# Five small edits to a two-block kernel: the last norm's totals, the keys' head sums, the gated outputs' split, a layer norm's mean, and gathered rows in the last inner units

## The chip, the cores and the metric

The kernel runs on one core of one Trainium2 chip. The metric is the device time of one execution in microseconds (us); lower is better. A core has five engines: TensorE (PE in the profile, with its weight loads as PEld), VectorE (DVE), ScalarE (ACT), GpSimd (POOL) and SyncE (SP, which here only issues loads and stores). Every engine runs its own list of instructions in order, and the engines wait for one another at semaphores.

## The reference

Two transformer blocks are applied to 256 tokens of width 2048, in float32:

```python
def first_block(x, mem, ...):      # one layer
    # k, v of memory = mem_n @ w_kv; rms norm of each of the 4 heads of q and of k; attention over 256 memory rows
    # gated delta rule on the projections; gates by silu; (gated outputs) @ w_out; residual
    ...
def second_block(x, ...):
    mix = jnp.concatenate([out_pool, out_attn], axis=-1) @ w_out[l]
    h = layer_norm(ALPHA * h + mix, ln1_g[l], ln1_b[l])
    ffn = peer_ffn(h, peer_wq[l], peer_subkeys[l], peer_u[l], peer_v[l])
    h = layer_norm(ALPHA * h + ffn, ln2_g[l], ln2_b[l])
```

`peer_ffn` lets every token choose experts by the sums of two top-k scores; a chosen expert contributes gelu(x·u) times its gate times its row v. The changed places are the norm of the memory's keys (`xa_k_norm_g`), the gated outputs ahead of `w_out`, the norm ln1, the last units of the products with u, and the norm ln2 that ends the kernel.

## The kernel before, in words

All weights come as 466 **units** of 128 x 2048 float32 (1 MB each), which SyncE loads into rotating buffers (`raw`). Float32 accuracy is kept by splitting: for each half unit ACT rounds 128 x 1024 values to a high part (`WH`, `cast`, L2619) and DVE subtracts that from the original to get the low part (`WL`, L1838). The activations are split in the same way, and PE forms three products, WH·XH, WH·XL and WL·XH (all at L1178). `do("prep", q)` splits half unit q; inside `unit` the half that is split is three halves ahead of the one that PE multiplies.

The class `Plan` writes one order of steps, and each engine emits its own part of each step, so that the order in `Plan.run` is the order on every engine. Side work is a generator that is advanced between the parts of a unit; `together(side, units, n)` advances both in turn. What a step waits for is written as `wait_ge(*at(name, count))`.

The places that the change touches, in order of time:

- **Memory's keys and values.** Units KV to KV+7 give the 8 key tiles, KV+8 to KV+15 the 8 value tiles. `head_norm("k")` runs beside the value units: `hn_square` (GpSimd multiplies 128 x 2048 keys by themselves, L3013), `hn_sum` (32 PE products 128 x 64 with a constant add the squares up; DVE takes the reciprocal of the root that ACT forms), `hn_spread`, `hn_apply`. `mv_root` is another small PE step after the second value unit.
- **Gated outputs.** Nine steps `y_split(c)` split 32 tiles of 128 x 256 in chunks of 2 to 4 tiles (`CHUNKS`; ACT casts L2795, DVE subtracts L2157) ahead of the units WO. The first chunk holds tiles 0 to 3, in the order in which WO's first unit uses them. The splits of half units that were asked for earlier stand behind these steps on both engines.
- **ln1.** `ln1` forms the mean MU and the reciprocal deviation RS of 256 tokens, and the product MR of both. `h2(c)` (c = 0 to 8) normalizes two of 16 row blocks a step (128 x 512): DVE multiplies by RS (L2307) and subtracts MR (L2309), ACT applies gain and bias (L2600) and casts (L2869), and one step later DVE subtracts the low part (L2313). Ahead of the steps stands `prep(2*WQ)` with the split of a half of unit WQ+1. The first two units of WQ follow as a pair.
- **PEER.** 192 of the 256 tokens take part in dense products over all experts: two halves, each with 64 inner units (u) and 64 outer units (v, `vm`). The last 64 tokens are done by rows that are gathered: `sp_gather(k)` is an indirect DMA of 128 rows, 1 MB, issued by GpSimd (L3197) into one of two buffers, and `sp_use(k)` a DVE operation 128 x 2048 on it (L1829 for the rows of v). `sp_gather(k)` waits for `sp_use(k-2)`. `pace` advances this side work by 0.13 or 0.05 of a step per part of an inner unit, and 0.27 or 0.3 per half of an outer unit (first or second half of PEER). An inner unit has 8 such parts. `c_begin(1)`, after the last inner unit, lets GpSimd issue three loads, 2 MB of the stored h and 1 MB each of ln2's gain and bias; they share one queue with the gathers.
- **End.** The two groups of 128 tokens (t = 0, 1) lie in `OUT[0]`, `OUT[1]`. For t = 0, DVE adds the four PSUM banks, ACT sums each row by a pass over the four parts (L2601); for t = 1 the rows of the last 64 tokens are brought to their place by 8 PE products, DVE copies the 64 others, ACT sums again. The mean goes to DVE, a pass `Square` with its row sum follows on ACT for each t, then one root of both (with an ACT table load before it), one reciprocal, and on DVE eight passes 128 x 1024 that subtract the mean, scale, and apply gain LG and bias LB. ACT and SyncE each issue two of the four output DMAs.

Of the kernel before, what the change touches and what calls it, by code (L numbers as in the profile page):

```python
# [149 lines left out]
CHUNKS = [list(range(4)), list(range(4, 8)), [10, 12, 14, 16], [18, 20, 22, 24], [26, 28, 30], [11, 13, 15, 17],  # L150
# [48 lines left out]
class Plan:  # L199
# [364 lines left out]
    def peer(self, half, st):  # L564
# [3 lines left out]
        for j in range(64):  # L568
# [5 lines left out]
            for _ in self.unit(PEER + 128 * half + j, per=6, later=later if half == 0 and j >= 62 else None):  # L574
# [9 lines left out]
                if half or j < 61:  # L584
                    self.pace(st, 2 * half)
# [32 lines left out]
    def run(self):  # L618
# [8 lines left out]
        for c in range(9):  # L627
            do("y_split", c)
# [43 lines left out]
        do("prep", 2 * WQ)  # L672
        for c in range(9):
            do("h2", c)
        do("sub_load")
# [24 lines left out]
def gate_counts():  # L700
# [14 lines left out]
    "x_high": (("n_hi", 32), ("y_hi", 9), ("x1_hi", 8), ("att_hi", 8), ("pm_hi", 8), ("h2_hi", 8)),  # L715
    "x_low": (("n_lo", 32), ("y_lo", 9), ("x1_lo", 8), ("att_lo", 8), ("pm_lo", 8), ("h2_lo", 8)),
# [35 lines left out]
def build(nc, D, out, scratch):  # L752
    ctx = ExitStack()
    with ctx:
# [30 lines left out]
        def f(kb, n):  # L785
            return view(kb, n, F)
# [245 lines left out]
        CM, MU, RS, MR = f(80, 256), f(81, 256), f(82, 256), f(83, 256)  # L1032
# [75 lines left out]
        def sync_program(e):  # L1108
# [51 lines left out]
            def end():  # L1160
                for p in range(2):
                    s.wait_ge(*at("out_t", 2 * p + 2))
# [661 lines left out]
        def vector_program(e):  # L1824
# [467 lines left out]
            def ln1():  # L2292
# [8 lines left out]
                v.wait_ge(*at("ln1_rs", 1))  # L2301
                v.step(tt(MR, MU, RS, ALU.mult))
# [153 lines left out]
            def sp_sum():  # L2456
# [6 lines left out]
                v.step(stt(x, HN[LAST, 2048:4096], ALPHA, x, ALU.mult, ALU.add))  # L2463
# [84 lines left out]
            def end():  # L2548
# [19 lines left out]
                v.wait_ge(*at("y2_sd", 1))  # L2568
                v.step(recip(stat(16, 2), stat(14, 2)))
                v.wait_ge(*at("ld_ln2", 32))  # L2570
                v.wait_ge(*at("y2_mean", 2))
                for t in range(2):
                    for c in range(2):
                        o = slice(1024 * c, 1024 * c + 1024)
                        x = OUT[t][:, o]
                        v.own()
                        v.step(stt(x, x, stat(10 + t), LG[:, o], ALU.add, ALU.mult))
                        v.own()
                        stt(x, x, stat(16 + t), LB[:, o], ALU.mult, ALU.add).then_inc(S["out_t"], 1)
# [15 lines left out]
        def scalar_program(e):  # L2595
# [378 lines left out]
            def end():  # L2974
                for t in range(2):
                    for d in range(4):
                        o = slice(d * 512, d * 512 + 512)
                        a.wait_ge(*at("y2", 4 * t + d + 1))
                        act(HN[:, t * 2048 + d * 512:t * 2048 + d * 512 + 512], OUT[t][:, o], ACT.Identity,
                            acc=stat(4 * t + d)).then_inc(S["y2_sum"], 1)  # L2980
                    a.wait_ge(*at("y2_mean", t + 1))
                    a.step(act(HN[:, t * 2048:t * 2048 + 2048], OUT[t], ACT.Square, bias=stat(10 + t), acc=stat(12 + t)))
                a.own()
# [332 lines left out]
```

## Time and profile before

| | |
|---|---|
| time, median of 3 runs | 2832.28 us (2826.26 to 2835.13) |
| profiled execution | 2836.36 us, of which the span from the first to the last instruction is 2834.5 us |
| PE busy | 2733.1 us, 96% of the span |
| DVE / ACT / POOL busy | 1929.7 us (68%) / 1384.3 us (49%) / 389.4 us (14%) |
| mean granted TensorE clock | 0.987 |
| PE's share of the chain that ended last | 73% (DVE 13%, DMA 7%, ACT 5%) |

PE's busy time is the sum of its matmul instructions; the rest of the span is idle time of PE, and the tail in which no product is left. The granted clock is the mean over the stretch of the clock that the chip gave TensorE, as a share of 2.4 GHz. A matmul in a stretch at 0.5 takes about twice as long. In timelines the time in brackets is the idle time of that engine just before the row, and behind the arrow stands what the profile infers to have ended it.

### The profile page before, as it was taken

How to read it: one execution, taken by the hardware profiler on the slowest of the kernel's cores; microseconds unless marked ns; L12 is line 12 of the kernel's file. 1: busy time of each engine (PE TensorE's matmuls, PEld its weight loads, DVE VectorE, ACT ScalarE, POOL GpSimd, SP SyncE). 2: the span in 40 equal slices, each digit the busy share in tenths (PEclk: the TensorE clock that was granted, in tenths of full speed). 3: DMA queues.
4: the chain of work that ended last, by engine and by line, in shares of the span. 5: the costliest groups of instructions: out<-in, count | busy, mean ns of one | idle time of the engine just before them, and what ended most of it. 6: DMA issues, size and time to landing. Idle time of an engine off the chain costs nothing.

```text
span 2834.5 us, 43483 instructions
## 1 busy us (share of the span) xinstructions
PE 2733.1 (96%) x17934; PEld 2557.6 (90%) x17934; DVE 1929.7 (68%) x2867; ACT 1384.3 (49%) x2255; POOL 389.4 (14%) x366
## 2 busy tenths in 40 slices
PE   8999989889999999999999999999999999999996
PEld 8899989889998889979989999998888999988885
DVE  7456578544445455564669657767888888878986
ACT  6356454556555444444453133435555555555554
POOL 0100020211110000005000012221222111113210
PEclk9999999999999999999999999999999999999998
DMA  6444455433335554544544579999999988899993
GB/s 256 163 150 163 149 164 185 140 104 117 102 114 193 193 181 166 189 157 151 179 149 149 202 268 346 359 346 366 377 378 380 345 319 322 324 353 367 371 365 123
DMA packets 109669, 668.28 MB, mean 236 GB/s; under 512 B 25777, under 2 KB 26313, under 8 KB 31553
## 3 DMA queue, kind: packets, MB, share of 16 engines
q1 hardware_dynamic: 83808, 496.08, 48.4%
q0 software_dynamic: 24512, 164.97, 16.0%
q10 hardware_dynamic: 1152, 4.47, 0.4%
q8 instruction: 142, 2.33, 0.3%
q14 instruction: 55, 0.44, 0.0%
HBM read 651.54 MB, written 13.30 MB: 235 GB/s over the span
## 4 chain that ended last, share of the span: by engine, by line
PE 73%; DVE 13%; DMA 7%; ACT 5%; issue 2%; POOL 0%; DVEq 0%; ACTq 0%
PE PS L1178 72%; DMA m<-in_pun,keep 4%; DVE WL L1838 4%; DVE m L1829 3%; ACT WH L2619 2%; DMA m<-in_pv,keep 1%; ACT m L2600 1%; PE PS L1181 1%; DVE m L2084 1%; ACT m L2601 1%; DMA m<-s_kk 1%; DVE m L2081 1%; PE PS L1556 0%; ACT L2600 0%; DVE m L2440 0%
## 5 line engine op out<-in xcount | busy, mean ns | idle before, releaser
L1838 DVE TENSOR_TENSOR WL<-raw,WH 128x1024 fp32r<-128x1024 f32 x708 | 869.0, 1233 | 544.8 <-ACT WH L2619 543.5
L2619 ACT CAST WH<-raw 128x1024 fp32r<-128x1024 f32 x708 | 736.8, 1046 | 393.5 <-PE PS L1178 381.0
L1178 PE MATMUL PS<-m_4096r,WH 128*128 128x256 f32 x4672 | 881.4, 289 | 12.1 <-DVE m L1829 5.2
L1178 PEld LDWEIGHTS PS<-m_4096r,WH 128*128 128x128 f32 x4672 | 734.3, 193 | 17.8 <-DVE m L1829 6.0
L1178 PE MATMUL PS<-m_4096r,WL 128*128 128x256 f32 x2336 | 663.6, 284 | 0.0
L1178 PE MATMUL PS<-WH,m_896r 128*128 128x512 f32 x1536 | 516.6, 390 | 6.5 <-DVE m_896r L2533 3.1
L1178 PEld LDWEIGHTS PS<-m_4096r,WL 128*128 128x128 f32 x2336 | 450.0, 193 | 0.0
L1178 PE MATMUL PS<-WL,m_896r 128*128 128x512 f32 x1024 | 399.1, 390 | 0.0
L1178 PE MATMUL PS<-m_8192r,WH 128*128 128x384 f32 (+1 forms) x1536 | 373.1, 331 | 8.2 <-issue 2.7
L1178 PEld LDWEIGHTS PS<-WH,m_896r 128*128 128x128 f32 x1536 | 289.0, 188 | 68.2 <-DVE m_896r L2533 4.2
L1178 PE MATMUL PS<-m,raw 128*128 128x192 f32 x2048 | 342.0, 326 | 0.0
L1178 PEld LDWEIGHTS PS<-m,raw 128*128 128x128 f32 x2048 | 331.6, 190 | 0.3 <-issue 0.2
L1178 PE MATMUL PS<-m_8192r,WL 128*128 128x192 f32 (+1 forms) x1280 | 258.8, 267 | 0.0
L1178 PEld LDWEIGHTS PS<-m_8192r,WH 128*128 128x128 f32 x1536 | 236.5, 193 | 10.4 <-issue 3.1
L1178 PEld LDWEIGHTS PS<-m_8192r,WL 128*128 128x128 f32 x1280 | 235.8, 190 | 0.0
L1178 PEld LDWEIGHTS PS<-WL,m_896r 128*128 128x128 f32 x1024 | 192.6, 188 | 39.9
L1178 PE MATMUL PS<-m 128*128 128x128 f32 (+2 forms) x1360 | 199.7, 285 | 27.8 <-ACT m L2600 18.1
L1178 PEld LDWEIGHTS PS<-m 128*128 128x128 f32 x1360 | 178.8, 194 | 34.0 <-ACT m L2600 19.5
L2440 DVE SCALAR_TENSOR_TENSOR m<-m 128x2048 f32<-128x2048 f32 x64 | 146.4, 2288 | 50.9 <-DMA m<-in_pun,keep 50.9
L3197 POOL DMA_INDIRECT m<-in_pv,keep x64 | 111.1, 1736 | 488.4 <-DVE m L1829 470.4
L1178 PE MATMUL PS<-WH,m_8192r 128*128 128x512 f32 x512 | 159.3, 392 | 2.7 <-issue 2.7
L1829 DVE SCALAR_TENSOR_TENSOR m<-m,keep 128x2048 f32<-128x2048 f32 (+1 forms) x67 | 152.9, 2283 | 7.5 <-DMA m<-in_pv,keep 7.2
(266 smaller groups left out, 2627.8 us busy)
## 6 DMA issues: line engine op xcount, KB each, us to landing
raw<-in_pu SPq DMA_DIRECT2D x112, 1024.0 KB, 7.1
raw<-in_pv SPq DMA_DIRECT2D x96, 1024.0 KB, 8.9
raw<-in_w_qkv SPq DMA_DIRECT2D x48, 1024.0 KB, 4.8
raw<-in_w_o SPq DMA_DIRECT2D x48, 1024.0 KB, 4.8
raw<-in_w SPq DMA_DIRECT2D x40, 1024.0 KB, 4.8
raw<-in_w_z SPq DMA_DIRECT2D x32, 1024.0 KB, 4.8
m<-in_pv SPq DMA_DIRECT2D x32, 1024.0 KB, 8.9
raw<-in_w_kv SPq DMA_DIRECT2D x16, 1024.0 KB, 5.2
```

The lines of the kernel that those rows point to most:

```text
L1178: return e.matmul(o, l, x, start=start, stop=stop)
L1181: return e.transpose(o, i, C("ident"))
L1829: return e.scalar_tensor_tensor(out=o, in0=a, scalar=s, in1=b, op0=op0, op1=op1)
L1838: tt(WL[:, k, :], raw_of(n)[:, h * 1024:h * 1024 + 1024], WH[:, k, :].bitcast(F), ALU.subtract).then_inc(S["lo"], 1)
L2081: v.step(tt(tmp, iv_u[:, :, c, j:j + 1].broadcast_to(shape), iv_e[:, 0:2, j:j + 1, r].broadcast_to(shape), ALU.mult))
L2084: t = tt(iv_u[:, :, c, r], iv_u[:, :, c, r], tmp, ALU.subtract)
L2440: x = e.scalar_tensor_tensor(out=g, in0=g, scalar=1.0, in1=XS, op0=ALU.mult, op1=ALU.mult, accum_out=DOT[:, r:r + 1])
L2600: return e.activation(o, i, fn, scale=scale, bias=bias)
L2601: return e.activation(o, i, fn, scale=scale, bias=bias, accum_out=acc)
L2619: e.copy(WH[:, k, :], raw_of(n)[:, h * 1024:h * 1024 + 1024]).then_inc(S["hi"], 1)
L3197: e.indirect_dma_start(out=GB[b], out_offset=None, in_=D["pun" if k < 64 else "pv"], in_offset=bass.IndirectOffsetOnAxis(ap=EI[:, r:r + 1] ...
```

## The change

The five edits:

- **Sums at the end (`end`).** For t = 0 the DVE additions also give the row sums; for t = 1 ACT copies the 64 rows out of PSUM and sums them, and the last 64 rows' sums come from the step that forms them (`sp_sum`). The root's table is loaded ahead by an operation on a constant, each t has its own root and reciprocal, and the second half of t = 1 is scaled by ACT and finished by GpSimd (times LG, plus LB), which SyncE's last store waits for.
- **Keys' head sums (`head_norm`).** For the keys two more `yield`s stand ahead of `hn_sum`, so that it and the steps after it come 8 parts, two units, later.
- **Gated outputs (`CHUNKS`).** Tiles 0 to 3 are split in three chunks of 1, 1 and 2 tiles rather than in one.
- **ln1's mean (`ln1`, `h2`).** GpSimd subtracts MU (a step per 128 x 512), DVE then multiplies by RS; MR is no longer formed. `prep(2*WQ)` stands behind `h2(3)` rather than ahead of `h2(0)`.
- **Gathered rows (`peer`).** In the inner units 61 to 63 of the second half `pace` is no longer called, as was already so in the first half.

```diff
-CHUNKS = [list(range(4)), list(range(4, 8)), [10, 12, 14, 16], [18, 20, 22, 24], [26, 28, 30], [11, 13, 15, 17],
+CHUNKS = [[0], [1], [2, 3], list(range(4, 8)), [10, 12, 14, 16], [18, 20, 22, 24], [26, 28, 30], [11, 13, 15, 17],
           [19, 21, 23, 25], [27, 29, 31], [8, 9]]
...
         self.do("hn_square", which)
         yield
         yield
+        if which == "k":
+            yield
+            yield
         self.do("hn_sum", which)
...
-                if half or j < 61:
+                if j < 61:
                     self.pace(st, 2 * half)
...
         do("ln1")
-        do("prep", 2 * WQ)
         for c in range(9):
             do("h2", c)
+            if c == 3:
+                do("prep", 2 * WQ)
...
             def h2(c):
                 if c < 8:
                     x = k3(X1)[:, 2 * c:2 * c + 2, :]
-                    a = v.step(tt(x, x, bc(RS, 2), ALU.mult))
-                    v.own(a)
-                    tt(x, x, bc(MR, 2), ALU.subtract).then_inc(S["h2_norm"], 1)
+                    v.wait_ge(*at("ln1_rs", 1))
+                    v.wait_ge(*at("h2_mean", c + 1))
+                    tt(x, x, bc(RS, 2), ALU.mult).then_inc(S["h2_norm"], 1)
...
+            def h2(c):
+                if c == 8:
+                    return
+                g_.wait_ge(*at("ln1_mu", 1))
+                x = k3(X1)[:, 2 * c:2 * c + 2, :]
+                tt(x, x, bc(MU, 2), ALU.subtract).then_inc(S["h2_mean"], 1)
...
                 v.wait_ge(*at("used", done(NUNIT - 1)))
+                for d in range(4):
+                    x = OUT[0][:, d * 512:d * 512 + 512]
+                    v.step(e.scalar_tensor_tensor(out=x, in0=x, scalar=1.0, in1=PS[:, d, :], op0=ALU.mult, op1=ALU.add,
+                                                  accum_out=stat(d)))
                 for t in range(2):
-                    for d in range(4):
-                        x = OUT[t][:, d * 512:d * 512 + 512]
-                        if t == 0:
-                            tt(x, x, PS[:, d, :], ALU.add).then_inc(S["y2"], 1)
-                        else:
-                            v.wait_ge(*at("folded", d + 1))
-                            copy(x[0:64, :], PS[0:64, 4 + d, :]).then_inc(S["y2"], 1)
-                    v.wait_ge(*at("y2_sum", 4 * t + 4))
+                    if t:
+                        v.wait_ge(*at("y2_copy", 4))
+                    v.own()
...
+                v.wait_ge(*at("y2_sd", 1))
+                v.step(recip(stat(16), stat(14)))
+                scaled(0, 0)
+                v.wait_ge(*at("y2_sd", 2))
+                v.step(recip(stat(17), stat(15)))
+                v.own()
+                tt(stat(18), stat(11), stat(17), ALU.mult).then_inc(S["y2_shift"], 1)
+                scaled(0, 1)
+                scaled(1, 0)
...
             def end():
+                act(stat(20), C("eps5"), ACT.Sqrt).then_inc(S["y2_table"], 1)
+                for d in range(4):
+                    a.wait_ge(*at("folded", d + 1))
+                    act(OUT[1][0:64, d * 512:d * 512 + 512], PS[0:64, 4 + d, :], ACT.Identity,
+                        acc=STAT[0:64, 4 + d:5 + d]).then_inc(S["y2_copy"], 1)
                 for t in range(2):
...
                     a.wait_ge(*at("y2_mean", t + 1))
                     a.step(act(HN[:, t * 2048:t * 2048 + 2048], OUT[t], ACT.Square, bias=stat(10 + t), acc=stat(12 + t)))
...
+                a.wait_ge(*at("y2_shift", 1))
+                act(OUT[1][:, 1024:2048], OUT[1][:, 1024:2048], ACT.Identity, scale=stat(17),
+                    bias=stat(18)).then_inc(S["y2_scaled"], 1)
...
+            def end():
+                x = OUT[1][:, 1024:2048]
+                g_.wait_ge(*at("y2_scaled", 1))
+                g_.wait_ge(*at("ld_ln2", 32))
+                g_.step(tt(x, x, LG[:, 1024:2048], ALU.mult))
+                g_.own()
+                tt(x, x, LB[:, 1024:2048], ALU.add).then_inc(S["out_pool"], 1)
```

How this moves instructions. On PE, after the products of the second value unit (`WH`, `WL` with the keys' and values' inputs in `m_4096r`), the head sums of the keys are the row with a constant and 128 x 64; before:

```order
L1178 MATMUL PS<-WH,m_4096r 128x512 x2
L1178 MATMUL PS<-WL,m_4096r 128x512
L1178 MATMUL PS<-cons,m_2048 128x64 x16
L1181 MATMUL PS<-cons,m_256 128x128 x2
L1178 MATMUL PS<-WH,m_4096r 128x512 x2
L1178 MATMUL PS<-WL,m_4096r 128x512
```

and of the change, at the same place:

```order
L1182 MATMUL PS<-WL,m_4096r 128x512
L1182 MATMUL PS<-WH,m_4096r 128x512 x2
L1182 MATMUL PS<-WL,m_4096r 128x512
L1185 MATMUL PS<-cons,m_256 128x128 x2
L1182 MATMUL PS<-WH,m_4096r 128x512 x2
L1182 MATMUL PS<-WL,m_4096r 128x512
```

The row with 128 x 64 is gone from here and stands two units of products further on, while the step `mv_root` (128 x 128) stays. On DVE, in ln1 and h2 (x is `m_4096`, MU, RS and MR are `m_256`), before:

```order
L2300 RECIPROCAL m_256<-m_256 128x256
L2302 TENSOR_TENSOR m_256<-m_256 128x256
L1838 TENSOR_TENSOR WL<-raw,WH 128x1024
L2307 TENSOR_TENSOR m_4096<-m_4096,m_256 128x512
L2309 TENSOR_TENSOR m_4096<-m_4096,m_256 128x512
L2307 TENSOR_TENSOR m_4096<-m_4096,m_256 128x512
L2309 TENSOR_TENSOR m_4096<-m_4096,m_256 128x512
L2313 TENSOR_TENSOR m_8192r<-m_4096,m_8192r 128x512
```

and of the change:

```order
L2304 RECIPROCAL m_256<-m_256 128x256
L2311 TENSOR_TENSOR m_4096<-m_4096,m_256 128x512 x2
L2315 TENSOR_TENSOR m_8192r<-m_4096,m_8192r 128x512
L2311 TENSOR_TENSOR m_4096<-m_4096,m_256 128x512
L2315 TENSOR_TENSOR m_8192r<-m_4096,m_8192r 128x512
L2311 TENSOR_TENSOR m_4096<-m_4096,m_256 128x512
L2315 TENSOR_TENSOR m_8192r<-m_4096,m_8192r 128x512
L1842 TENSOR_TENSOR WL<-raw,WH 128x1024
L2311 TENSOR_TENSOR m_4096<-m_4096,m_256 128x512
```

One DVE operation of two per piece is gone, and the weight split stands behind the fourth multiplication, ahead of the fourth low part. On GpSimd, around the three loads of `c_begin(1)` (`in_pv` rows are the gathers), before and of the change:

```order
L3197 DMA m_2048<-in_pv,keep 128x2048 x26
L3227 DMA m_4096<-s_h 128x4096
L3228 DMA m_2048<-in_ln2g 128x2048
L3229 DMA m_2048<-in_ln2b 128x2048
L3197 DMA m_2048<-in_pv,keep 128x2048 x30
```

```order
L3218 DMA m_2048<-in_pv,keep 128x2048 x24
L3248 DMA m_4096<-s_h 128x4096
L3249 DMA m_2048<-in_ln2g 128x2048
L3250 DMA m_2048<-in_ln2b 128x2048
L3218 DMA m_2048<-in_pv,keep 128x2048 x32
```

Two gathers that stood ahead of the three loads now stand behind them in the queue.

## Rows read from the trace of the kernel before

**Rows 1.** Part 1 of the page: busy time, share of the span, instructions.

```profile
PE 2733.1 (96%) x17934; PEld 2557.6 (90%) x17934; DVE 1929.7 (68%) x2867; ACT 1384.3 (49%) x2255; POOL 389.4 (14%) x366
```

**Rows 2.** Timeline of PE, rows with idle time: start, us, instruction, [idle before].

```profile
78.53 6.84 PE L1178 MATMUL PS<-cons,m 128*128 128x64 f32 x32 [3.38 <-POOL m L3013]
...
867.41 1.19 PE L1178 MATMUL PS<-WH,m_8192r 128*128 128x512 f32 x2 [2.71 <-issue]
...
1433.48 0.48 PE L1178 MATMUL PS<-m_8192r,WH 128*128 128x256 f32 x2 [2.71 <-issue]
...
2512.90 0.80 PE L1178 MATMUL PS<-WH,m_896r 128*128 128x512 f32 x1 [2.75 <-DVE cons L2525]
...
2543.94 0.50 PE L1178 MATMUL PS<-WH,m_896r 128*128 128x512 f32 x1 [2.11 <-DVE m_896r L2533]
```

**Rows 3.** Stretches: us; busy PE, PEld, DVE, ACT, POOL (count); PEclk; DMA share; GB/s.

```profile
78.91:89.15 10.24, 10.24 (x42) 9.47 (x42) 1.51 (x3) 1.20 (x2) 0.00 (x0) 0.50 0.08 10
...
1434.00:1437.40 3.40, 3.40 (x18) 3.40 (x18) 3.35 (x6) 2.74 (x6) 0.00 (x0) 0.51 0.00 0
```

**Rows 4.** Timeline of PE: the same 32 products for the queries.

```profile
184.65 3.68 PE L1178 MATMUL PS<-cons,m 128*128 128x64 f32 x32
```

**Rows 5.** Timelines of POOL and DVE around GpSimd's two multiplications 128 x 2048.

```profile
70.57 7.91 POOL L3013 TENSOR_TENSOR m<-m 128x2048 f32<-128x2048 f32 x1 [70.12 <-DVE m L1901]
...
70.39 4.62 DVE L1838 TENSOR_TENSOR WL<-raw,WH 128x1024 fp32r<-128x1024 f32 x4
...
175.94 3.60 POOL L3013 TENSOR_TENSOR m<-m 128x2048 f32<-128x2048 f32 x1 [97.46 <-ACT m L2680]
...
176.84 3.78 DVE L1838 TENSOR_TENSOR WL<-raw,WH 128x1024 fp32r<-128x1024 f32 x1 [1.87 <-ACT WH L2619]
```

**Rows 6.** Timelines of ACT and DVE ahead of unit WO.

```profile
865.01 7.76 ACT L2795 CAST m_8192r<-m 128x1024 fp32r<-128x1024 f32 x9
...
866.08 9.24 DVE L2157 TENSOR_TENSOR m_8192r<-m,m_8192r 128x1024 fp32r<-128x1024 f32 x9 [1.87 <-ACT m_8192r L2795]
875.24 4.63 DVE L1838 TENSOR_TENSOR WL<-raw,WH 128x1024 fp32r<-128x1024 f32 x4
```

**Rows 7.** Timeline of DVE in h2: the early split, the first and the last low part.

```profile
1428.34 1.22 DVE L1838 TENSOR_TENSOR WL<-raw,WH 128x1024 fp32r<-128x1024 f32 x1
...
1432.69 0.69 DVE L2313 TENSOR_TENSOR m_8192r<-m,m_8192r 128x512 fp32r<-128x512 f32 x1 [0.48 <-ACT m_8192r L2869]
...
1446.18 0.69 DVE L2313 TENSOR_TENSOR m_8192r<-m,m_8192r 128x512 fp32r<-128x512 f32 x1 [1.21 <-ACT m_8192r L2869]
```

**Rows 8.** GpSimd's groups: count, busy us, mean ns, idle before and its releaser.

```profile
L3040 POOL TENSOR_TENSOR m<-m,m 128x512 f32<-128x512 f32 x12 | 15.3, 1278 | 49.5 <-ACT m L2600 49.5
```

**Rows 9.** Timelines of DVE and POOL, then DMA issues 2480 to 2580 us (count, size, us to landing).

```profile
2541.27 2.35 DVE L1829 SCALAR_TENSOR_TENSOR m<-m,keep 128x2048 f32<-128x2048 f32 x1 [3.83 <-DMA m<-in_pv,keep]
...
2524.45 1.73 POOL L3197 DMA_INDIRECT m<-in_pv,keep  x1 [8.85 <-DVE m L1829]
...
m<-s_h POOLq DMA_DIRECT2D x1, 2048.0 KB, 11.1
...
m<-in_ln2b POOLq DMA_DIRECT2D x1, 1024.0 KB, 21.2
```

**Rows 10.** Timelines of PE, ACT and DVE at the end.

```profile
2808.57 3.65 PE L1178 MATMUL PS<-m,cons 128*64 128x512 f32 x8
...
2817.33 2.00 ACT L2601 ACTIVATE m<-m,keep 128x2048 f32<-128x2048 f32 x1 [0.41 <-DVE keep L1832]
...
2819.44 1.28 ACT L2600 ACT_TABLE_LOAD   x1
2820.73 0.29 ACT L2600 ACTIVATE keep<-keep,cons 128x2 f32<-128x2 f32 x1
...
2821.36 5.12 DVE L1829 SCALAR_TENSOR_TENSOR m<-m,keep,m 128x1024 f32<-128x1024 f32 x4
2826.40 5.12 DVE L1829 SCALAR_TENSOR_TENSOR m<-m,keep 128x1024 f32<-128x1024 f32 x4
```

More of the change, by code:

```diff
@@ L626, in run @@
         self.mix()
-        for c in range(9):
+        for c in range(len(CHUNKS)):
             do("y_split", c)
@@ L1161, in end @@
                 for p in range(2):
-                    s.wait_ge(*at("out_t", 2 * p + 2))
+                    s.wait_ge(*at("out_pool", 1) if p else at("out_t", 2))
                     e.dma_start(out[0, tok(p), 1024:2048], OUT[p][:, 1024:2048]).then_inc(S["st_sync"], 16)
@@ L2462, in sp_sum @@
                 v.wait_ge(*at("ld_hn", 16))
-                v.step(stt(x, HN[LAST, 2048:4096], ALPHA, x, ALU.mult, ALU.add))
+                v.step(e.scalar_tensor_tensor(out=x, in0=HN[LAST, 2048:4096], scalar=ALPHA, in1=x, op0=ALU.mult, op1=ALU.add,
+                                              accum_out=STAT[LAST, 4:5]))
+                v.step(copy(STAT[LAST, 5:8], C("zero")[LAST, 0:3]))
             count = {"gelu": 0, "gated": 0, "apply": 0}
@@ L2567, in end, with scaled @@
                     one(stat(10 + t), stat(8 + t), -1.0 / 2048, ALU.mult).then_inc(S["y2_mean"], 1)
-                v.wait_ge(*at("y2_sd", 1))
-                v.step(recip(stat(16, 2), stat(14, 2)))
                 v.wait_ge(*at("ld_ln2", 32))
                 v.wait_ge(*at("y2_mean", 2))
[L2572 to L2579, printed above, removed]
+                def scaled(t, c):
+                    o = slice(1024 * c, 1024 * c + 1024)
+                    x = OUT[t][:, o]
+                    v.own()
+                    v.step(stt(x, x, stat(10 + t), LG[:, o], ALU.add, ALU.mult))
+                    v.own()
+                    stt(x, x, stat(16 + t), LB[:, o], ALU.mult, ALU.add).then_inc(S["out_t"], 1)
+                v.wait_ge(*at("y2_sd", 1))
[3 more added lines that the diff above has]
+                v.step(recip(stat(17), stat(15)))
+                v.own()
+                tt(stat(18), stat(11), stat(17), ALU.mult).then_inc(S["y2_shift"], 1)
+                scaled(0, 1)
+                scaled(1, 0)
             Plan({"prep": prep, "begin": begin, "m_split": m_split, "n_add": n_add, "n_root": n_root, "n_scale": n_scale,
@@ L2974, in end @@
             def end():
-                for t in range(2):
[L2976 to L2980, printed above, removed]
+                act(stat(20), C("eps5"), ACT.Sqrt).then_inc(S["y2_table"], 1)
[3 more added lines that the diff above has]
+                        acc=STAT[0:64, 4 + d:5 + d]).then_inc(S["y2_copy"], 1)
+                for t in range(2):
                     a.wait_ge(*at("y2_mean", t + 1))
                     a.step(act(HN[:, t * 2048:t * 2048 + 2048], OUT[t], ACT.Square, bias=stat(10 + t), acc=stat(12 + t)))
-                a.own()
-                act(stat(14, 2), stat(12, 2), ACT.Sqrt, scale=1.0 / 2048, bias=C("eps5")).then_inc(S["y2_sd"], 1)
+                    a.own()
+                    act(stat(14 + t), stat(12 + t), ACT.Sqrt, scale=1.0 / 2048, bias=C("eps5")).then_inc(S["y2_sd"], 1)
+                a.wait_ge(*at("y2_shift", 1))
+                act(OUT[1][:, 1024:2048], OUT[1][:, 1024:2048], ACT.Identity, scale=stat(17),
+                    bias=stat(18)).then_inc(S["y2_scaled"], 1)
                 for t in range(2):
@@ L3114, in x_load @@
             def x_load():
-                g_.wait_ge(*at("y_lo", 9))
+                g_.wait_ge(*at("y_lo", len(CHUNKS)))
                 e.dma_start(f(120, 4096), D["x"]).then_inc(S["ld_res"], 16)
             def bias_load():
-                g_.wait_ge(*at("y_lo", 9))
+                g_.wait_ge(*at("y_lo", len(CHUNKS)))
                 g_.wait_ge(*at("used", done(KIWI - 1)))
@@ L3229, in c_begin @@
                 e.dma_start(LB, D["ln2b"]).then_inc(S["ld_ln2"], 16)
-            Plan({"hn_square": hn_square, "qk_out": qk_out, "iv_turn": iv_turn, "iv_store": iv_store,
+            def end():
[5 more added lines that the diff above has]
+                tt(x, x, LB[:, 1024:2048], ALU.add).then_inc(S["out_pool"], 1)
+            Plan({"end": end, "hn_square": hn_square, "qk_out": qk_out, "iv_turn": iv_turn, "iv_store": iv_store,
                   "iv_scale": iv_scale, "iv_out": iv_out, "dn_low": dn_low, "dn_y": dn_y, "gate": gate, "x_load": x_load, "bias_load": bias_load, "bias": bias, "ki_out": ki_out,
-                  "pool_loads": pool_loads, "pu_out": pu_out, "sub_load": sub_load, "h_store": h_store,
+                  "pool_loads": pool_loads, "pu_out": pu_out, "h2": h2, "sub_load": sub_load, "h_store": h_store,
                   "c_begin": c_begin, "s_add": s_add, "g_apply": g_apply, "gate_load": gate_load,
```

8 lines of the change are left out of this document (3 added, 5 removed).

## The prediction, made before the changed kernel had run

> **What bounds the kernel now.** I read the page's busy times first. PE is busy for 2733.1 us [rows 1], 96% of the span of 2834.5 us, and no edit takes a product away. So an edit can only pay where PE idles, where it runs at a low clock, or behind the last product. I then read PE's timeline at the changed places for idle time [rows 2]. PE waits 3.38 us ahead of the keys' head sums, 2.71 us ahead of the first product with the gated outputs, 2.71 us ahead of the first product of WQ, and 2.75 us after the last inner unit. A further gap of 2.11 us at 2543.94 is in the outer units, at a gathered row. Together that is 13.7 us.
>
> The clock adds to some of these. A table by stretches shows PE granted 0.50 from 78.91 to 89.15 and 0.51 from 1434.00 to 1437.40 [rows 3], which is the level of 1.2 GHz. At 2512.90 one product 128x512 takes 0.80 us, at 2543.94 the same product takes 0.50 [rows 2]: after the 2.75 us gap the clock was low, after the 2.11 us gap it was not. So a gap of nearly three microseconds costs its length and, when the clock falls with it, some 1.7 us more (half of the 3.40 us in rows 3).
>
> **Keys' head sums.** PE waits for GpSimd's multiplication, which takes 7.91 us because it runs beside four DVE subtractions [rows 5]. It ends at 78.48, and 78.53 is when the 32 products start [rows 2]. Moved two units, the sums are asked for about 11 us later (two units of products, an estimate of 5 to 6 us each from the timeline ahead), at some 86 us, so 3.38 us of wait go. The cover is the weights split already: DVE finishes four half units by 75.01 (70.39 + 4.62, rows 5), and these are what PE multiplies in place of the sums. The 32 products take 6.84 us at half clock [rows 2]; the queries' same 32 take 3.68 us at full clock [rows 4]. That is 3.16 us. The stretch at half clock runs on to 89.15 [rows 3]: from 85.4 on, 3.7 us of ordinary products that would take half, some 1.7 us less. Sum +8.2 us. The low bound is 3.4 us, if the 32 short products bring the clock down wherever they stand; rows 4 speak against that. High bound 8.5. What is late next: the reciprocal, the spread and the scaled keys, two units later; nothing reads them before the attention over memory, behind all value units. On DVE the reciprocal waits with the next weight split behind it, for the 4 us that the sums and the root take; the split is three halves ahead, so this is hidden.
>
> **Gated outputs.** Nine casts take 7.76 us and nine subtractions 9.24 us [rows 6], or 0.86 and 1.03 each, so the first chunk of four tiles costs 1.9 us before PE can start at 867.41. A quarter of it would take about 0.6 us, so PE starts some 1.3 us earlier. But the low part that the second half of WO's second unit needs is among the four subtractions that start at 875.24 [rows 6], behind all chunks on DVE. The tiles are the same 32, so DVE comes there at the same time, or 0.1 us later for two more instructions. PE gets there 1.3 us sooner and waits longer. I take 0. If the clock falls in that new wait, −1.7; if PE never catches up with DVE there, +1.3.
>
> **ln1's mean.** Before, DVE does three operations 128x512 per piece, and low parts come every 1.93 us (1432.69 to 1446.18, seven steps, rows 7). Of the change DVE does two, 2 x 0.69 = 1.38, and GpSimd one. GpSimd's nearest row is 128x512 in 1.28 us [rows 8]. Can the two overlap? Rows 5 say no. The multiplication that ran beside four subtractions took 7.91 us, the one that ran with one waiting took 3.60 us; the difference of 4.3 is about the time of the subtractions, and the one that waited took 3.78 us where such a one takes 1.22 [rows 7]. Then a piece costs 1.28 + 1.38 = 2.66 us, 0.73 more than before. GpSimd starts when the mean is there, ahead of DVE's reciprocal, so I count three of the eight pieces as done ahead: 5 x 0.73 = 3.7 us later. Against it, 1.22 us of the split and one 0.69 us operation no longer stand ahead of the first low part: 1.9 us sooner. The split is now behind the fourth piece, where the low part of that piece queues behind it on DVE while it waits for ACT's cast; PE will show a gap there, but the pieces behind come from GpSimd's head start. I take −1.8 us. Bounds: all eight pieces later and the split in full, 5.8 + 1.2 − 1.9 = −5.1; with no exclusion, +1.9 less what the split gives back, so +1.5.
>
> **Gathered rows.** Without the row ahead of the last inner unit's sum (a DVE operation of 2.35 us, as in rows 9), the gap of 2.75 us shrinks to about 0.8 and the clock should hold: 1.9 + 1.6 = +3.5 us. But the 24 parts are 1.2 steps of the side work, and two gathers now stand behind 4 MB of loads in GpSimd's queue. The last of these loads lands 21.2 us after its issue, and the gather issued at 2524.45 behind them landed only at 2541.27, 16.8 us later where the median is 10.1 [rows 9]. That cost DVE 3.83 us and PE 2.11 us. In the change a gather issued at about 2518 stands in that place, needed by about 2527 (the order puts this DVE operation in the fourth outer unit). It lands at 2533 to 2535, so DVE stalls for 6 to 7.5 us. Weight splits wait behind it, 1.5 units ahead; PE's gap, 2.11 before, would be 3.2 to 4.7, perhaps with the clock. That takes back 1 to 4.3 us. I take +0.5; bounds −2.5 and +3.5.
>
> **The end.** The last of eight DVE passes ends at 2831.52 (2826.40 + 5.12, rows 10), and 3.0 us more go to the last store. PE's last product ends at 2812.22. Of the change, ACT's last copy of 64x512 ends about 0.7 us behind that (a quarter of a 2.00 us pass and its readout). Then Square 2.1, root 0.3, reciprocal 0.2: 2815.6, where before the reciprocal came after both squares, the table load and the root, at 2821.06. Two passes at 1.27 (10.16 us for eight, rows 10) end at 2818.2. The second reciprocal and shift end at 2818.6, and ACT's scaling of 128x1024, half of 2.00, at 2819.8. What is left is four DVE passes, 5.1 us, and two GpSimd operations 128x1024. The latter are not in the trace: from 128x512 they are 2.56 us each [rows 8], from 128x2048 1.80 [rows 5]; I take 2.3, so 4.6. Each has two inputs from memory, as rows 5 have, so by those rows they exclude DVE's: 2818.6 + 5.1 + 4.6 = 2828.3. Gain +3.2 us. If they overlap, 2819.8 + 4.6 = 2824.4, gain 7.1; if GpSimd stretches 2.2 times, as 7.91 to 3.60, 2829.9, gain 1.6.
>
> The table load off the path is 1.28 us of this: the root starts at 2820.73, with nothing between it and the load [rows 10]. The Trainium skill (ScalarE: Activation LUTs, "What ACT_TABLE_LOAD costs") gives 1283 ns for the load, which this trace agrees with, and another 1380 ns for a drain, which it does not show. By the page the gain at the end would be an estimated 1.4 us larger.
>
> **Sum.** 8.2 + 0 − 1.8 + 0.5 + 3.2 = +10.1 us. The profiled execution took 2836.36 us, so it would take 2826.3. It lies 4.1 us above the median of 2832.28, inside the runs' 2826.26 to 2835.13; against the median the forecast is 2832.28 − 10.1 = 2822.2 us. Some 0.3%, 8.5 us, is what a measurement of this kernel can tell from no change.
>
> **Rivals.**
> - *Nothing excludes, and no new gap.* GpSimd's subtraction is hidden (+1.5), the end gains 7.1, the gathered rows 3.5, the gated outputs 1.3, the head sums 8.2: 21.6 at the most; with one of these missing, about 17, so 2815 us. For it: GpSimd is busy for 14% only. Against it: rows 5, twice.
> - *The late gather and the short products.* The 32 products bring their own low clock (gain 3.4 rather than 8.2), or the stall in the outer units takes all that the inner unit gave and 2.5 more. Either leaves 5 to 7 us, 2825 to 2827 us: no change that can be told. For it: a queue that answers in 16.8 us [rows 9]. Against it: rows 4.
> - *GpSimd stretched in ln1: slower than before.* If GpSimd's 1.28 us per piece stretches as in rows 5, to 2.8, and DVE's 1.38 comes on top, a piece takes 4.2 us: 8 x (4.2 − 1.93) − 1.9 = 16.3 us lost rather than 1.8, so the sum is −4.4, 2836.7 us. It decides from (10.1 + 1.8 + 1.9)/8 above 1.93, some 3.65 us per piece. For it: the 7.91 us. Against it: there DVE had four operations ready, in h2 it waits for GpSimd at each piece, so GpSimd finds the way free. The Trainium skill (GPSIMD Engine Reference, "Specifications") says that GpSimd's interfaces to the memory are shared with VectorE, and contended by instructions with two such inputs; the trace agrees by the 7.91 us, and that section puts no figure on it.
> - *The gated outputs' new wait* is in the terms already, by at most 1.7.
>
> **Chances and range.** My forecast, gains of 6 to 14 us, has 0.60; the large gain 0.13; the small gain 0.20; slower 0.07. Of the forecast's case some seven tenths lie above 8.5 us, so faster is 0.60 x 0.7 + 0.13 = 0.55; slower by over 0.3% needs the third rival with low clock in its gaps, 0.03; the rest is 0.42. The range runs from the large gain to the small one, 2814 to 2831 us.
>
> **What the trace will show.** Right: no gap at 74.9 us and granted clock 1.0 to 89 us, with 32 products in about 3.7 us near 86; PE starting on WO near 866 and waiting around 875; POOL rows of 1.3 us or more in h2 and low parts about 2.7 us apart, with one PE gap after the fourth piece; a gap under 1 us at the last inner unit and a longer one about four outer units later; a last DVE or POOL operation near 2828. Wrong: a low clock at the head sums in their new place; low parts under 2 us or over 3.6 us apart; DVE and POOL passes overlapping at the end; a gathered row that DVE does not wait for.

## The result, and the profile after

The changed kernel takes 2836.84 us in the median of 18 runs (2828.59 to 2846.58), the one before 2827.45 us over the 18 runs taken with and before it (2818.73 to 2835.13). The ratio is 1.0033, 95% interval 1.0024 to 1.0042: slower by 9.4 us, where 10 us faster was forecast. The three runs of before that the forecast had show a median of 2832.28 us, and its profiled execution, 2836.36 us, lies above all of these 18, and above the three runs' highest of 2835.13, where the prediction has it inside them. So the forecast counted from a time that was some 5 us too long: 10.1 us off the 2827.45 would have been 2817.4.

The profiled execution of the changed kernel has a span of 2836.8 us and took 2838.57 us. Its part 1 answers to [rows 1]:

```profile
PE 2733.8 (96%) x17934; PEld 2558.6 (90%) x17934; DVE 1932.6 (68%) x2862; ACT 1382.9 (49%) x2252; POOL 404.7 (14%) x376
```

Products and their time are the same, so all is in idle time, clock and tail. PE's timeline at the places of [rows 2], with idle time in brackets:

```profile
864.21 0.70 PE L1182 MATMUL PS<-WH,m_8192r 128*128 128x512 f32 x2 [1.61 <-issue]
...
874.41 0.73 PE L1182 MATMUL PS<-WH,m_8192r 128*128 128x512 f32 x2 [1.78 <-DVE WL L1842]
...
1432.72 0.76 PE L1182 MATMUL PS<-m_8192r,WH 128*128 128x256 f32 x2 [2.99 <-issue]
...
1441.84 0.50 PE L1182 MATMUL PS<-m_8192r,WH 128*128 128x256 f32 x2 [1.53 <-DVE m_8192r L2315]
...
2509.37 0.50 PE L1182 MATMUL PS<-WH,m_896r 128*128 128x512 f32 x1 [0.80 <-DVE cons L2529]
...
2540.22 0.79 PE L1182 MATMUL PS<-WH,m_896r 128*128 128x512 f32 x1 [7.88 <-DVE m_896r L2537]
```

The wait of 3.38 us at the keys' sums is gone, the gap after the last inner unit fell from 2.75 to 0.80 us, and the first product of WO starts after 1.61 us rather than 2.71. Against that stand new or longer gaps: 1.78 at 874.41, 1.53 at 1441.84, and 7.88 at 2540.22 where it was 2.11. The end is in DVE's and GpSimd's timelines and in the instructions of the program's last line (engine queue, operation: duration in ns, start in us):

```profile
2822.53 6.64 DVE L1833 SCALAR_TENSOR_TENSOR m<-m,keep 128x1024 f32<-128x1024 f32 x2
...
2821.46 3.35 POOL L3256 TENSOR_TENSOR m<-m 128x1024 f32<-128x1024 f32 x1 [46.41 <-ACT m L2611]
2824.90 3.19 POOL L3258 TENSOR_TENSOR m<-m 128x1024 f32<-128x1024 f32 x1
...
L758 POOLq DRAIN  x1: 11658/11658/11658, 2824.9 to 2824.9; - x1
L758 SPq DRAIN  x1: 7/7/7, 2832.3 to 2832.3; - x1
```

DVE's last pass ends at 2829.17, GpSimd's last operation at 2828.09, the last products' start being 1.65 us later than before. Counted from the last products' start, the passes are through 4 us sooner than in [rows 10]. But GpSimd's drain, the instruction behind its last operation, begins with that operation and ends at 2836.6, 8.5 us behind it. SyncE, the last of the others, was through at 2832.3; the span ends at 2836.8, with the drain. Before, its drain began at 2763.9 and was over long ahead of the end.

### The profile page after: what moved, and what is told of

It reads as the page before. It is cut to its first block, busy times and chain, and to the rows that moved or that the text cites. A ratio compares the mean times of both kernels' runs of the same rounds, so it can differ in the third digit from the quotient of the medians.

```text
span 2836.8 us, 43488 instructions
## 1 busy us (share of the span) xinstructions
PE 2733.8 (96%) x17934; PEld 2558.6 (90%) x17934; DVE 1932.6 (68%) x2862; ACT 1382.9 (49%) x2252; POOL 404.7 (14%) x376
## 4 chain that ended last, share of the span: by engine, by line
PE 80%; DVE 12%; ACT 5%; DMA 2%; issue 1%; POOL 0%; ACTq 0%; DVEq 0%
PE PS L1182 79%; DVE WL L1842 4%; DVE m L1833 2%; ACT WH L2630 2%; ACT m L2611 1%; PE PS L1185 1%; DMA m<-in_pv,keep 1%; DVE m L2088 1%; DMA m<-s_kk 1%; PE PS L1560 1%; DVE m L2085 1%; ACT L2611 0%; ACT m_4096r L2611 0%; ACT m L2612 0%; DVE m L2325 0%
## 5 line engine op out<-in xcount | busy, mean ns | idle before, releaser
L1833 DVE SCALAR_TENSOR_TENSOR m<-m,keep 128x2048 f32<-128x2048 f32 (+1 forms) x65 | 154.4, 2375 | 12.6 <-DMA m<-in_pv,keep 12.6
```

What stands on the lines that cost most here:

```text
L1833: return e.scalar_tensor_tensor(out=o, in0=a, scalar=s, in1=b, op0=op0, op1=op1)
```

## The experiments

Ratios are to runs of the kernel before beside them, with 95% intervals; 1.001 is 2.8 us. Stretches are taken from PE's timeline between the same products in each trace: they tell what one edit does to its own place more sharply than the whole time, which scatters by some 4 us between executions.

**The gathered rows alone, twice.**

```diff
-                if half or j < 61:
+                if j < 61:
                     self.pace(st, 2 * half)
```

> The kernel before with the edit on the gathered rows alone (no pacing in the inner units 61 to 63 of the second half). Theory 1 (the late gather is the loss): the gap of 2.75 us after the last inner unit shrinks to about 0.8 us, and a DVE operation on a gathered row waits about 10 us in the outer units, PE with it for 7 to 8 us where it was 2.11; 3 to 6 us slower than before, ratio 1.001 to 1.002. Rival (the late gather was one execution's accident): the stall is 4 us or less and the edit is 2 to 3.5 us faster.

> The edit on the gathered rows alone, again. Theory 1: a PE gap of 6 to 8 us some 30 us after the first outer product, in place of about 2 us, less the 1.95 us gained ahead of it: 1 to 4 us slower than before. Rival (the gained gap and clock pay for the late gather): 1 us slower to 2 us faster.

Ratios 1.0008 (0.9993 to 1.0024) and 0.9990 (0.9974 to 1.0006). Both profiles show the gap of 0.80 us ahead of the outer units and PE gaps of 6.39 and 6.62 us in them; from the first outer product to the last rows' products it takes 298.9 and 300.4 us, against a mean of 296.2 over twelve profiles of kernels without this edit (293.5 to 302.5). The mechanism of theory 1 is there both times. Its net cost, 1 to 2 us by the stretches (300.4 − 296.2, less the 1.95 us gained ahead, is the larger), is within the scatter of the whole times, so that 0 cannot be excluded.

**The gathered rows, with two of the loads later.**

```diff
+            if half and j in (12, 20):
+                self.do("ln2_load", j)
...
-                e.dma_start(LG, D["ln2g"]).then_inc(S["ld_ln2"], 16)
-                e.dma_start(LB, D["ln2b"]).then_inc(S["ld_ln2"], 16)
+            def ln2_load(j):
+                e.dma_start(*((LG, D["ln2g"]) if j == 12 else (LB, D["ln2b"]))).then_inc(S["ld_ln2"], 16)
```

> The kernel before with the edit on the gathered rows, and with the loads of the last norm's gain and bias (1 MB each) moved from the start of the outer units to the outer units 12 and 20; the 2 MB of h stay. Theory 1 (the gathers are late because 4 MB stand ahead of them in GpSimd's queue): PE's gap in the outer units, 6 to 8 us with the edit alone, falls to 2.5 us or less, and the kernel is 1 to 3 us faster than before. Rival (the two gathers themselves are late, whatever stands ahead): a gap of 5 us or more stays.

Ratio 0.9978 (0.9963 to 0.9993), some 6 us faster where 1 to 3 were expected. The gap at the late row is gone altogether, and the stretch is the shortest of all, 291.4 us. So the loads ahead in GpSimd's queue made the gathers late. How late, the changed kernel's GpSimd, DVE and DMA issues (2500 to 2560 us; size, us to landing) show: the gather issued at 2514.77, behind the three loads of 2508.87 to 2510.53, is used at 2536.41.

```profile
2509.97 0.56 POOL L3250 DMA_DIRECT2D m<-in_ln2b  x1
2514.77 1.73 POOL L3218 DMA_INDIRECT m<-in_pv,keep  x1 [4.25 <-DVE m L1833]
...
2536.41 2.35 DVE L1833 SCALAR_TENSOR_TENSOR m<-m,keep 128x2048 f32<-128x2048 f32 x1 [10.40 <-DMA m<-in_pv,keep]
...
m<-in_ln2b POOLq DMA_DIRECT2D x1, 1024.0 KB, 21.5
```

The three loads land 12.6, 17.0 and 21.5 us after their issues, at about 2521.5, 2526.4 and 2531.5, and the gather 4.9 us behind the last of them: one after the other in the order of issue, each of the last three MB some 5 us behind the one before. Before, too, the gather landed 5.1 us behind the third load (issued at 2515.02, landed 21.2 us later [rows 9]).

**The end alone, twice.** (The hunks of `end` and `sp_sum`.)

```diff
+                scaled(0, 1)
+                scaled(1, 0)
...
+                g_.step(tt(x, x, LG[:, 1024:2048], ALU.mult))
+                g_.own()
+                tt(x, x, LB[:, 1024:2048], ALU.add).then_inc(S["out_pool"], 1)
```

> The kernel before with the edits at the end alone (sums by additions, roots apart, GpSimd finishes the last quarter). Theory 1 (GpSimd's drain at the end eats the gain): DVE and GpSimd are done 23 us or less after the start of the eight products 128x512 that bring the last rows to their place, but the span ends only some 8 us after GpSimd's last operation, about 26.5 us after these products' start where it was 25.9; no change to 1 us slower. Rival: the drain is as short as it was in the kernel before, and the edit gains 2 to 3 us.

> The edits at the end alone, again. Theory 1 (nothing outside the tail): 0 to 3 us slower than before, and the time from the first outer unit's first product to the last products is that of the kernels without this edit, 294 to 299 us. Rival (the edit also slows the outer units): 5 us or more slower, and that time is 301 us or more, as in the first profile (302.5).

Ratios 1.0022 (1.0004 to 1.0039) and 1.0000 (0.9986 to 1.0014). The tail, from the start of the last rows' products to the end of the span, is 26.55 and 26.50 us, against 25.93 in the profiled kernel before. Theory 1 holds for the tail. The rival that the edit also slows the outer units fell: their stretch was 302.5 us in the first profile and 295.5 in the second.

**The end without GpSimd, twice.** DVE does the last quarter as a fourth `scaled` (the main lines against the kernel of the end alone; ACT's and GpSimd's parts of the last quarter go too).

```diff
-                tt(stat(18), stat(11), stat(17), ALU.mult).then_inc(S["y2_shift"], 1)
                 scaled(0, 1)
                 scaled(1, 0)
+                scaled(1, 1)
```

> The kernel before with the edits at the end, but without GpSimd: DVE does the last quarter too, ACT's scaling and GpSimd's step are left out. Theory 1 (GpSimd's drain costs about 8 us behind its last operation): the span ends some 20.5 us after the start of the eight products for the last rows, where it was 25.9 before and 26.6 with GpSimd. Rival (the passes themselves set the end, GpSimd's drain only fills a wait): DVE's two further passes bring the end to 26 us or more.

> The edits at the end without GpSimd, again. Theory 1 (nothing outside the tail): 4 to 7 us faster than before, 5 to 7 us faster than with GpSimd in this same call. Rival (the outer units are slowed too): 0 to 3 us faster.

Ratios 0.9968 (0.9954 to 0.9983) and 0.9976 (0.9965 to 0.9986); the tail is 20.44 us in both, 6.1 less than with GpSimd. Of these, some 4.3 us are the drain (from SyncE's 2832.3 to GpSimd's 2836.6 in the changed kernel) and the rest the slower passes. The wish to spare DVE two passes cost the whole gain of this edit.

**One short GpSimd addition behind the last pass.**

```diff
+            def end():
+                g_.wait_ge(*at("out_t", 4))
+                tt(stat(20), stat(0), stat(1), ALU.add).then_inc(S["tiny"], 1)
```

> The kernel before with one GpSimd addition of 128x1 behind the last DVE pass; its result is not used. Theory 1 (the drain is a fixed time of GpSimd after whatever it did last): the span ends about 8.5 us after this addition, 31 to 32 us after the start of the products for the last rows, where it was 25.9. Rival (the drain belonged to the long 128x1024 operations): the span ends at 26 to 27 us, with the last store.

The tail is 31.91 us, 6 more than before, for an addition of 0.20 us. GpSimd's timeline, and its drain in the last line's instructions:

```profile
2818.41 0.20 POOL L3233 TENSOR_TENSOR keep<-keep 128x1 f32<-128x1 f32 x1 [67.16 <-DVE m L1829]
...
L754 POOLq DRAIN  x1: 8662/8662/8662, 2818.4 to 2818.4; - x1
```

The drain ends 8.46 us behind the addition, as it ended 8.47 us (11.658 − 3.19) behind the long operation in the changed kernel: the length of the operation does not matter. It is not the same behind everything. Where GpSimd's last act is to issue a DMA, as in the kernel before, the drain ended 10.4 to 14.9 us behind that issue in 15 profiles, at 2783.9 at the latest, where it delays nothing.

**The keys' head sums alone.**

```diff
+        if which == "k":
+            yield
+            yield
         self.do("hn_sum", which)
```

> The kernel before with the keys' head sums two units later and nothing else. Theory 1: no wait at the sums and no low clock there, PE is 6 to 7 us further at 200 us, and stays so: 5 to 7 us faster, ratio about 0.998. Rival (the clock takes it back): PE's gaps after 390 us are the same, but the clock falls in more of them, and by 560 us the lead is 2 us or less; no change.

Ratio 1.0001 (0.9985 to 1.0018), neither as theory 1 nor by the rival's mechanism. The other profiles tell why. In e_end, whose code up to there is that of before, the same place reads (PE, then GpSimd and DVE):

```profile
75.05 3.79 PE L1178 MATMUL PS<-cons,m 128*128 128x64 f32 x32
...
70.48 4.51 POOL L3025 TENSOR_TENSOR m<-m 128x2048 f32<-128x2048 f32 x1 [70.03 <-DVE m L1901]
...
70.32 8.02 DVE L1838 TENSOR_TENSOR WL<-raw,WH 128x1024 fp32r<-128x1024 f32 x4
```

No wait, and no low clock: here DVE was held up (8.02 us for four subtractions, where [rows 5] have 4.62) and GpSimd came through in 4.51 us. In e_mean, again the old code at this place, GpSimd was held up as in the profile of before:

```profile
78.35 7.09 PE L1179 MATMUL PS<-cons,m 128*128 128x64 f32 x32 [3.39 <-POOL m L3012]
...
70.39 7.91 POOL L3012 TENSOR_TENSOR m<-m 128x2048 f32<-128x2048 f32 x1 [69.94 <-DVE m L1902]
```

Which of the two engines wins is settled anew in each execution: one and the same kernel gave 6.77 us for GpSimd in e_rows and 4.51 in e_rows_2, and 7.91 in e_mean and 4.51 in e_mean_2. Of 14 profiles with the old place of the sums, three have the wait of 3.4 us, one of 0.63 and ten none. The queries' sums behind it start at 184.1 to 184.7 us in the three, at 176.3 to 178.8 in the others, 178.9 in the mean; in six profiles with the new place at 177.2 to 177.8, 177.5 in the mean. By these means the edit is worth 1.4 us, not 8.2; the scatter of the 14 leaves it uncertain by some 2 us.

**The layer norm's mean alone, twice, and with the split left ahead.**

```diff
-        do("prep", 2 * WQ)
         for c in range(9):
             do("h2", c)
+            if c == 3:
+                do("prep", 2 * WQ)
```

> The kernel before with the layer norm's mean by GpSimd and the split moved, nothing else. Theory 1 (GpSimd and DVE exclude each other, and the moved split makes a gap): the pair of the first two units of WQ ends 2 to 3 us later, 2 to 3 us slower. Rival (GpSimd's part is hidden, and the gap in the changed kernel is the clock's): 0 to 1.5 us faster.

> The layer norm's mean by GpSimd and the moved split alone, again. Theory 1 (nothing outside its stretch): 2 to 5 us slower than before. Rival: 6 us or more slower.

> The kernel before with the layer norm's mean by GpSimd, and the weight split left where it was, ahead of the first piece. Theory 1 (both the exclusion and the moved split cost): the first products of WQ start 2 us or less after the constant products, and the first two units of WQ take 17 to 18 us from their first product to the first product behind them, where it was 16.8 before and 19.8 with the split moved. Rival (all of the loss is the exclusion): 19.5 us or more here too. Second rival (all of it is the moved split): 16.8 or less.

Ratios 1.0025 (1.0003 to 1.0047) and 1.0010 (0.9995 to 1.0025). PE waits 2.98 and 2.99 us ahead of WQ's first product (2.71 before), and from that product to the first behind the pair takes 19.80 and 19.88 us against 16.78: 3.3 us lost in this place. With `prep` left where it was (the diff above undone), the first wait is 3.97 us and the pair takes 16.49: 1.0 us lost. That is one profile, and none of its three expectations fits: the pair is as short as the second rival had it, and the loss is in the wait ahead. So GpSimd's part costs 1 us and the moved split 2.3. The changed kernel's GpSimd and DVE show both:

```profile
1423.39 12.06 POOL L3184 TENSOR_TENSOR m<-m,m 128x512 f32<-128x512 f32 x8 [103.96 <-ACT m L2611]
...
1432.54 1.76 DVE L2311 TENSOR_TENSOR m<-m,m 128x512 f32<-128x512 f32 x1
1434.23 1.77 DVE L2315 TENSOR_TENSOR m_8192r<-m,m_8192r 128x512 fp32r<-128x512 f32 x1
1435.92 0.68 DVE L2311 TENSOR_TENSOR m<-m,m 128x512 f32<-128x512 f32 x1
...
1439.36 1.23 DVE L1842 TENSOR_TENSOR WL<-raw,WH 128x1024 fp32r<-128x1024 f32 x1 [2.16 <-ACT WH L2630]
```

GpSimd runs through its eight pieces in 12.06 us, without a pause, at 1.3 to 1.5 us each before DVE's multiplications begin and 1.72 beside them. While it does, DVE's operations take 1.76 us, the 0.68 of the third row and the rest of a GpSimd operation. Then DVE stands still for 2.16 us ahead of the moved split, with the low part of the fourth piece behind it.

**The finer chunks alone.**

```diff
-CHUNKS = [list(range(4)), list(range(4, 8)), [10, 12, 14, 16], [18, 20, 22, 24], [26, 28, 30], [11, 13, 15, 17],
+CHUNKS = [[0], [1], [2, 3], list(range(4, 8)), [10, 12, 14, 16], [18, 20, 22, 24], [26, 28, 30], [11, 13, 15, 17],
```

> The kernel before with the finer chunks of the gated outputs alone. Theory 1: PE starts on WO 1.1 us sooner, waits some 1.8 us for the weights' low part at the second unit's second half, and its clock falls there too; from 820 to 1430 us of the program PE loses 1 to 2 us. Rival (the forecast's 0): the head start is handed back and nothing more, 0 to 0.3 us.

Ratio 0.9995 (0.9980 to 1.0011). PE waits 1.61 us rather than 2.71 ahead of WO and then 1.78 at the second unit, as in the changed kernel. But here the clock held in that wait, and from WO's first product to WQ's takes 566.6 us, 0.5 more than the 566.1 of before, with a start 1.1 sooner: 0.6 us gained. In the three profiles with all edits it takes 568.5, of which 0.3 is the layer norm's first wait. There the clock fell each time (0.57 to 0.60 over the 4 us behind the wait). The stretch behind the wait in the changed kernel, then in e_chunks (columns as in [rows 3]):

```profile
874.60:878.60 4.00, 4.00 (x12) 3.11 (x12) 3.16 (x3) 0.07 (x1) 0.00 (x0) 0.60 0.94 319
```

```profile
868.70:872.70 4.00, 4.00 (x18) 3.31 (x19) 3.21 (x4) 1.15 (x2) 0.00 (x0) 1.00 0.99 270
```

The same wait, at 0.60 and at 1.00 of the clock: 12 and 18 products in 4 us, the first mostly at the level of 1.2 GHz. With the low clock the edit loses 1.1 us.

**All edits again, and all with the end by DVE.** The second has the edit of e_end_dve in the changed kernel.

> The changed kernel as it is, again, beside the others of this call. Theory 1 (the parts add up, with the keys' wait taken at its mean of some 2 us over the executions seen): 3 to 6 us slower than before. Rival (something beyond the parts, as the first comparison's 9 us hints): 8 us or more slower on this chip too. In its profile the drain of GpSimd ends the span some 8.5 us after its last operation, whichever.

> The changed kernel, but DVE does the last quarter and GpSimd ends with its last load, as in e_end_dve. Theory 1: the tail behind the last products is 20.5 us rather than 26.6, and the kernel is 6 us faster than the changed one, within 2 us of before. Rival (GpSimd's drain is hidden in most executions): within 2 us of the changed kernel.

Ratios 1.0034 (1.0022 to 1.0045) and 1.0017 (1.0007 to 1.0028): the first result stands in a second measurement, 9.6 us slower, as the rival had it and not 3 to 6. GpSimd's part in the end accounts for half of it, 4.8 us (the tails are 26.56 and 20.39 us); the other half stays, so the version with the end by DVE is not within 2 us of before, as theory 1 had it, but 4.8 us slower.

**Versions that beat both kernels.** e_best: the keys' sums later, the end by DVE, the rows with spread loads; e_best_2 leaves out the keys' edit, e_best_3 the rows and loads.

> The keys' head sums later, the sums at the end without GpSimd, and the gathered rows with the two loads spread; the gated outputs and the layer norm's mean as before. Theory 1 (the parts add up): 5.5 us from the end, 2 from the keys' wait, 1 to 3 from the rows: 8 to 11 us faster than before, ratio 0.996 to 0.997. Rival (the outer units give back what the inner unit gained, since their transfers are the limit there): 5 to 7 us faster.

> The end without GpSimd and the gathered rows with the two loads spread; keys' head sums as before. Theory 1 (the keys' edit is worth its mean, some 2 us): 7 to 10 us faster than before, 1 to 4 us slower than the version with the keys' edit (0.9963). Rival (the keys' edit is worth nothing in most executions): 0.9963 or below here too.

> The end without GpSimd and the keys' head sums later; the gathered rows and their loads as before. Theory 1 (the parts add up: 5.5 us of the tail, some 2 of the keys): 6 to 9 us faster than before, 0.997 to 0.998, and slower than with the rows and spread loads as well (0.9963). Rival (the spread loads add nothing, since the transfers limit the outer units): as fast as with them, 0.9965 or below.

Ratios 0.9963 (0.9949 to 0.9977), 0.9977 (0.9964 to 0.9989) and 0.9964 (0.9947 to 0.9980). The best is 10 us faster than before and 20 us faster than the changed kernel. The end by DVE carries most of it. The spread loads, good for 6 us alone, add nothing that can be told to it: in the outer units these versions took 294.0, 302.3 and 294.8 us, and why e_best_2 lost 6 us there, in two gaps of PE that DVE's late gathers bring, is not known. So its time does not say what the keys' edit is worth.

## Why the prediction was wrong

**The end: the first step that failed.** "3.0 us more go to the last store" was carried over from before as what follows the last operation. It follows DVE's or ACT's last operation; behind GpSimd's comes its drain of 8.5 us. The rest of that step came out near: the exclusion ("they exclude DVE's") is seen in DVE's two last passes, 6.64 us for two against [rows 10]'s 5.12 for four, and in GpSimd's operations, 3.35 and 3.19 us beside them rather than 2.3; and the passes end at 2829.2, 15.3 us behind the last product, where the forecast had 16.1. Forecast +3.2, measured −0.6, which without the 4.3 us of the drain would be an estimated +3.7; without GpSimd +5.5.

**The keys' sums: the largest error.** The mechanism was read rightly, and the wait and the low clock do vanish. But the step took the profiled execution as typical. It was one of three in 14 in which GpSimd had to wait for all four of DVE's subtractions. "These are what PE multiplies in place of the sums" held; the gain is 1.4 us in the mean, not 8.2: in ten of the 14 there was no wait to remove. That the same rows carried a contest between two engines was in [rows 5]; that its outcome may differ from one execution to the next should have lowered the price. The Trainium skill (SBUF — State Buffer, "SBUF: two separate sides") calls the shared port pair an exclusive lock that the one who starts first gets for the whole instruction. The traces agree that the one is held up for the whole of the other's instruction: 4.51 us for GpSimd go with a DVE subtraction of 4.62. That the first to start gets it is not seen in the profile's start times: in all 20 profiles GpSimd starts 0.16 to 0.18 us behind DVE's first subtraction and some 0.96 ahead of the second, and yet in five of them the second and third went ahead of it. By the traces' nanoseconds these five start 171 to 175 ns behind the first subtraction, the fifteen others 163 to 170; whether that decides it, no run tested.

**The layer norm's mean: sign right, size off.** Forecast −1.8, measured −3.3, within the bounds. "A piece costs 1.28 + 1.38" is too little while GpSimd has pieces left, when each of DVE's two operations takes 1.76 us, and too much afterwards; GpSimd found the way free, as the third rival's counter-argument had it, and ran ahead. By the runs GpSimd's part costs 1 us. The term that was mis-sized is the split behind the fourth piece: counted as a gain ahead and a gap that GpSimd's head start makes good, it costs 2.3 us.

**The gathered rows: mechanism right, size off.** The gap of 0.80 us came as forecast ("shrinks to about 0.8"), the late row waited for 10.4 us instead of 6 to 7.5, PE for 6.4 to 7.9 us instead of 3.2 to 4.7. The gather landed 21.6 us after its issue; the step took 15 to 17, carried over from the one of before (16.8), which was issued later behind the same loads. But the landing goes by the loads: both gathers came some 5 us behind the third load, so the earlier issue only waited longer. Forecast +0.5, by the stretches −1 to −2, by the whole times about 0.

**The gated outputs: held,** with its own reservation: 0 forecast, +0.6 or, with the clock, −1.1.

**The sum.** By the stretches of the profiles with all edits (at the end those of the changed kernel's code): −0.6 for the end, +1.4 keys (the mean), −3 mean, −3 rows (301 against 296.2, less 1.95), −1.1 chunks, so some 6 us slower. Two measurements of the whole say 9.4 and 9.6. The single edits' ratios, averaged where there are two, give 0.0011 for the end + 0.0001 keys + 0.0018 mean − 0.0001 rows − 0.0005 chunks, that is some 7 us, each uncertain by 3 to 5. The three or so microseconds between are not settled. A single profile cannot settle them: from the queries' sums to WO, where only the chunks change anything, and that by 1.1, the 20 profiles take 679.2 to 687.5 us. None of the rivals had the drain; the range missed mainly because of it and of the execution that was taken for the rule.

## What to carry to other kernels

Before an engine is given work at the very end, look at what its last instruction does after it: here a GpSimd operation that ended 4.2 or 2.5 us before the last of the other engines was through moved the end, whether it took 3.19 or 0.20 us. A wait that stems from two engines contending for a port is a draw, not a fixed cost: look at several executions before pricing its removal. When side work is moved past loads on the same in-order queue, count the bytes that it now stands behind: here some 5 us for each MB. Spreading them alone brought 6 us, the move itself none that could be told.

## What the runs showed that was not expected

- GpSimd's drain at the end of the program ends 8.46 us after a 0.20 us addition and 8.47 us after a 3.19 us operation, but 10.4 to 14.9 us after the issue of a DMA.
- One and the same pair, a GpSimd multiplication 128x2048 beside four DVE subtractions, gives 4.51, 6.77 or 7.91 us for GpSimd in executions whose code up to there is the same.
- A wait of 1.78 us, with the same work behind it, was followed by a granted clock of 0.57 to 0.60 in the three profiles with all edits and of 1.00 in that of the chunks alone.
